# Rope of the second block: the rotation matmul replaced by four quarter evictions on ScalarE

## The reference, cut to what matters

```python
D_MODEL = 1024; SEQ = 256; ROT_DIM = 16
DA_HEADS = 8; DA_HEAD_DIM = 64; DIL_HEADS = 12; DIL_HEAD_DIM = 64

def partial_rope(t, cos, sin):
    half = ROT_DIM // 2
    t1, t2, tp = t[..., :half], t[..., half:ROT_DIM], t[..., ROT_DIM:]
    return jnp.concatenate([t1 * cos - t2 * sin, t2 * cos + t1 * sin, tp], axis=-1)

def second_block(x, positions, w_in, ...):
    cos, sin = rope_tables(positions, x.dtype)
    x = x + 0.5 * rmsnorm(swiglu(rmsnorm(x, g_pre_ffn1), w_gu1, w_down1), g_post_ffn1)
    h = rmsnorm(x, g_pre_mix)
    z = h @ w_in
    qa, ka, va, qd, kd, vd, ga, gb = jnp.split(z, cuts, axis=-1)   # 1024,1024,1024,768,768,768,1024,1024
    qa = partial_rope(qa.reshape(B, S, 2 * DA_HEADS, DA_HEAD_DIM), cos, sin)
    ka = partial_rope(ka.reshape(B, S, 2 * DA_HEADS, DA_HEAD_DIM), cos, sin)
    ...
    qd = partial_rope(qd.reshape(B, S, DIL_HEADS, DIL_HEAD_DIM), cos, sin)
    kd = partial_rope(kd.reshape(B, S, DIL_HEADS, DIL_HEAD_DIM), cos, sin)
    ...
```

## Time and profile before

| | |
|---|---|
| median of three runs | 1683.3 us (1682.68 to 1686.57) |
| the profiled execution, its own time | 1685.99 us |
| its span | 1684.2 us |
| TensorE (PE) busy | 1607.2 us, 95% |
| VectorE (DVE) busy | 1113.2 us, 66% |
| ScalarE (ACT) busy | 701.9 us, 42% |
| mean granted TensorE clock | 0.983 |

### The profile page before, as it was taken

One profiled execution on the slowest core, in us unless ns is written; L12 is line 12 of the kernel. 1 busy time (PEld: TensorE's weight loads), 2 busy tenths in 40 slices (PEclk: granted clock), 3 DMA queues, 4 the chain that ended last, 5 costly groups with the idle time before them and its releaser, 6 DMA issues.

```text
span 1684.2 us, 22878 instructions
## 1 busy us (share of the span) xinstructions
PE 1607.2 (95%) x9150; PEld 1334.4 (79%) x9150; DVE 1113.2 (66%) x1370; ACT 701.9 (42%) x889; POOL 53.0 (3%) x103
## 2 busy tenths in 40 slices
PE   6999999999999998999999999998999898889998
PEld 4655658888787877688999889997999787878887
DVE  4446526688888757457676788766664775557776
ACT  3425325222222236355444644344333554454343
POOL 1150000000000000000000000000000000000000
PEclk9999999999999999999999999998999999999999
DMA  9730462444565323113655566553555223426552
GB/s 394 282 116 1 157 225 75 150 150 152 182 240 200 125 75 100 51 57 133 202 176 186 163 201 198 176 189 103 157 159 173 93 77 100 161 77 206 192 182 92
DMA packets 168314, 258.16 MB, mean 153 GB/s; under 512 B 4176, under 2 KB 147024, under 8 KB 161456
## 3 DMA queue, kind: packets, MB, share of 16 engines
q1 hardware_dynamic: 160720, 205.21, 36.9%
q0 software_dynamic: 7376, 51.65, 8.2%
q10 hardware_dynamic: 144, 0.26, 0.1%
HBM read 256.05 MB, written 1.05 MB: 153 GB/s over the span
## 4 chain that ended last, share of the span: by engine, by line
PE 85%; issue 5%; DVE 4%; ACT 3%; DMA 2%; POOL 0%; DVEq 0%; SPq 0%; ACTq 0%
PE psum L355 52%; PE psum L375 14%; PE psum L379 7%; PE psum L476 2%; DMA U<-in_mod_pieces 1%; PE psum L1083 1%; PE psum L641 1%; DMA U<-in_w_mod 1%; PE psum L1124 1%; PE psum L2116 1%; PE psum L2388 1%; ACT w_hi L333 1%; PE psum L2367 1%; DVE scr L509 1%; PE psum L2200 1%
## 5 line engine op out<-in xcount | busy, mean ns | idle before, releaser
L337 DVE TENSOR_TENSOR w_lo<-w_raw,w_hi 128x2048 fp32r<-128x2048 f32 x189 | 432.8, 2290 | 184.9 <-ACT w_hi L333 183.3
L333 ACT ACTIVATE w_hi<-w_raw 128x2048 fp32r<-128x2048 f32 x189 | 360.8, 1911 | 260.0 <-PE psum L355 199.9
L355 PE MATMUL psum<-h_hi,w_hi 128*128 128x256 f32 (+1 forms) x1120 | 389.5, 348 | 19.9 <-DVE h_lo L522 9.3
L375 PE MATMUL psum<-h_hi,w_hi 128*128 128x512 f32 x1056 | 378.0, 401 | 11.9 <-DVE h_hi L490 7.6
L355 PE MATMUL psum<-h_lo,w_hi 128*128 128x256 f32 (+1 forms) x1120 | 375.9, 336 | 0.0
L355 PE MATMUL psum<-h_hi,w_lo 128*128 128x256 f32 (+1 forms) x1120 | 375.9, 336 | 0.0
L379 PE MATMUL psum<-h_hi,w_lo 128*128 128x256 f32 x1056 | 297.8, 282 | 0.0
L355 PEld LDWEIGHTS psum<-h_hi,w_hi 128*128 128x128 f32 x1120 | 216.8, 194 | 64.6 <-issue 33.5
L375 PEld LDWEIGHTS psum<-h_hi,w_hi 128*128 128x128 f32 x1056 | 200.0, 189 | 62.3 <-issue 14.0
L355 PEld LDWEIGHTS psum<-h_lo,w_hi 128*128 128x128 f32 x1120 | 217.2, 194 | 23.4 <-issue 4.1
L355 PEld LDWEIGHTS psum<-h_hi,w_lo 128*128 128x128 f32 x1120 | 216.8, 194 | 20.8
(11 more groups left out here) (294 smaller groups left out, 1703.0 us busy)
## 6 DMA issues: line engine op xcount, KB each, us to landing
w_raw<-in_ffn_w_up SPq DMA_DIRECT2D x44, 1024.0 KB, 5.1
w_raw<-in_w_gu SPq DMA_DIRECT2D x44, 1024.0 KB, 5.1
U<-in_w_mod POOLq DMA_DIRECT2D x40, 1024.0 KB, 5.5
w_raw<-in_w_in SPq DMA_DIRECT2D x29, 1024.0 KB, 5.3
w_raw<-in_ffn_w_down SPq DMA_DIRECT2D x22, 1024.0 KB, 5.0
w_raw<-in_w_down SPq DMA_DIRECT2D x22, 1024.0 KB, 5.0
U<-in_mod_pieces POOLq DMA_DIRECT2D x8, 1024.0 KB, 18.0
w_raw<-in_gqa_w_in SPq DMA_DIRECT2D x6, 1024.0 KB, 5.1
```

What stands on the lines that cost most here:

```text
L333: nc.scalar.activation(w_hi[:, i % RING, :], w_raw[:, i % RING, :], ACT.Copy).then_inc(hi_made, 1)
L337: nc.vector.tensor_tensor(w_lo[:, i % RING, :], w_raw[:, i % RING, :], w_hi[:, i % RING, :].bitcast(F32), ALU.subtract).then_inc(lo_made, 1)
L355: return [nc.tensor.matmul(dst, x, y, start=start and q == 0, stop=stop and q == 2, skip_group_check=True) for q, (x, y) in enumerate(pairs)]
L375: made = nc.tensor.matmul(psum[:, bank, :], wh, h_hi[:, k, :], start=k == 0, stop=False, skip_group_check=True)
```

## The change

The columns of the query and key weights are put in another order by the host (`qk_columns`): within each head of 64, numbers 0 to 7 stay at 0 to 7, numbers 16 to 39 come next, numbers 8 to 15 (the partners) go to places 32 to 39, and the rest follows. Partners are then exactly 32 partitions apart, and the exchange of partners is an exchange of neighbouring groups of 32 partitions. ScalarE makes it while it empties the PSUM bank: four instructions, each of 32 partitions x 512, which read group q ^ 1 and write group q of `scr`. The sign goes into the frequencies, so that the sine table is negative for one of the partners. VectorE then multiplies the bank itself by cosine (into `t_rope`), the swapped copy by sine, and adds. The matmul with `rot_b2` and its matrix in `const` are gone, VectorE handles stripe u in its own turn rather than one turn later, and the products go round six PSUM banks rather than four.

```diff
-    add("qkv", columns("w_in_2", 0, qk + v))
+    add("qkv", columns("qk_columns", 0, range(0, 3584, 256)) + columns("w_in_2", 0, v))
...
-        const = sb("const", [P, 5 * P + 8])
+        const = sb("const", [P, 4 * P + 8])
...
         def qkv_tensor(pe):
-            def turn(v):
-                pe.wait_ge(r_evac, v + 1)
-                need(pe, r_fix, 3 * (v - 1))
-                nc.tensor.matmul(psum[:, 4 + v % 2, :], rot_b2, t_rope[:, v % 2, :], start=True,
-                                 stop=True).then_inc(r_rot, 1)
-
...
-                need(pe, r_evac, u - 3)
+                need(pe, r_evac, u - 5)
+                need(pe, r_fix, 3 * (min(u - 6, N_ROT - 1) + 1))
                 for t in range(2):
-                    dst, done = psum[:, u % 4, block_cols(t)], r_sums if t else None
+                    dst, done = psum[:, u % 6, block_cols(t)], r_sums if t else None
...
-                if 1 <= u <= N_ROT:
-                    turn(u - 1)
 
         def qkv_scalar(act):
...
                 if u < N_ROT:
                     need(act, r_fix, 3 * (u - 1))
-                    nc.scalar.activation(t_rope[:, u % 2, :], psum[:, u % 4, :], ACT.Copy).then_inc(r_evac, 1)
+                    for q in range(4):
+                        made = nc.scalar.activation(scr[32 * q:32 * q + 32, u % 2, :],
+                                                    psum[32 * (q ^ 1):32 * (q ^ 1) + 32, u % 6, :], ACT.Copy)
+                    made.then_inc(r_evac, 1)
...
         def qkv_vector(dve):
...
-                if not 1 <= u <= N_ROT:
+                if u >= N_ROT:
                     continue
-                v = u - 1
-                dve.wait_ge(r_rot, v + 1)
-                need(dve, r_fix, 3 * v - 3)
-                x = t_rope[:, v % 2, :].rearrange("p (s t) -> p s t", s=2)
-                tmp = scr[:, v % 2, :].rearrange("p (s t) -> p s t", s=2)
-                nc.vector.tensor_tensor(tmp, bank2(4 + v % 2), double(tab_b2[:, 1, :]), ALU.mult).then_inc(r_fix, 1)
-                nc.vector.tensor_tensor(x, x, double(tab_b2[:, 0, :]), ALU.mult).then_inc(r_fix, 1)
-                dve.wait_ge(r_fix, 3 * v + 2)
-                nc.vector.tensor_tensor(qkv_dst(v), x, tmp, ALU.add).then_inc(r_fix, 1)
+                dve.wait_ge(r_evac, u + 1)
+                need(dve, r_fix, 3 * u - 3)
+                x = t_rope[:, u % 2, :].rearrange("p (s t) -> p s t", s=2)
+                other = scr[:, u % 2, :].rearrange("p (s t) -> p s t", s=2)
+                nc.vector.tensor_tensor(x, bank2(u % 6), double(tab_b2[:, 0, :]), ALU.mult).then_inc(r_fix, 1)
+                nc.vector.tensor_tensor(other, other, double(tab_b2[:, 1, :]), ALU.mult).then_inc(r_fix, 1)
+                dve.wait_ge(r_fix, 3 * u + 2)
+                nc.vector.tensor_tensor(qkv_dst(u), x, other, ALU.add).then_inc(r_fix, 1)
...
-            sp.dma_start(const[:, 0:5 * P + 3], a["const_base"]).then_inc(base_in, 16)
+            sp.dma_start(const[:, 0:4 * P + 3], a["const_base"]).then_inc(base_in, 16)
...
+    order = np.r_[0:8, 16:40, 8:16, 40:64]
+    qk_columns = np.concatenate([w_in_2[:, :, 0:2048], w_in_2[:, :, 3072:4608]], 2)
+    qk_columns = qk_columns.reshape(1, D, -1, 64)[:, :, :, order].reshape(1, D, -1)
```

More of the change, by code:

```diff
@@ L75, in stripes @@
     add("ffn2", ffn("w_gu1_2", "w_down1_2", 0))
-    qk = [*range(0, 2048, 256), *range(3072, 3840, 256), *range(3840, 4608, 256)]
     v = [*range(2048, 3072, 256), *range(4608, 5376, 256)]
-    add("qkv", columns("w_in_2", 0, qk + v))
+    add("qkv", columns("qk_columns", 0, range(0, 3584, 256)) + columns("w_in_2", 0, v))
     gate_b = columns("w_in_2", 0, range(6400, 7424, 256))
@@ L122, in build @@
         rinv = sb("rinv", [P, TT])
-        const = sb("const", [P, 5 * P + 8])
-        group_sum = const[:, 5 * P + 1:5 * P + 3]
+        const = sb("const", [P, 4 * P + 8])
+        group_sum = const[:, 4 * P + 1:4 * P + 3]
         par = sb("par", [P, 4, P])
@@ L132, in build @@
         ident, ones = const[:, 0:P], const[:, P:2 * P]
-        rot_mla, rot_gqa, rot_b2 = (const[:, i * P:(i + 1) * P] for i in (2, 3, 4))
-        inv_freq = const[:, 5 * P:5 * P + 1]
+        rot_mla, rot_gqa = (const[:, i * P:(i + 1) * P] for i in (2, 3))
+        inv_freq = const[:, 4 * P:4 * P + 1]
         eps, eps_down = small_w[:, 0:1], small_w[:, 1:2]
@@ L2140, in qkv_scalar @@
                     need(act, r_fix, 3 * (u - 1))
-                    nc.scalar.activation(t_rope[:, u % 2, :], psum[:, u % 4, :], ACT.Copy).then_inc(r_evac, 1)
+                    for q in range(4):
+                        made = nc.scalar.activation(scr[32 * q:32 * q + 32, u % 2, :],
+                                                    psum[32 * (q ^ 1):32 * (q ^ 1) + 32, u % 6, :], ACT.Copy)
+                    made.then_inc(r_evac, 1)
                 else:
-                    nc.scalar.activation(qkv_dst(u), bank2(u % 4), ACT.Copy).then_inc(r_evac, 1)
+                    nc.scalar.activation(qkv_dst(u), bank2(u % 6), ACT.Copy).then_inc(r_evac, 1)
         def qkv_vector(dve):
@@ L2738, in shape_constants @@
     f = np.float32
-    base = np.zeros((P, 5 * P + 3), f)
+    base = np.zeros((P, 4 * P + 3), f)
     base[:, 0:P] = np.eye(P)
     base[:, P:2 * P] = 1
-    rot = np.zeros((3, P, P), f)
+    rot = np.zeros((2, P, P), f)
     for which, rows in ((0, range(NOPE, MLA_QK, 2)), (1, range(0, P, 2))):
@@ L2745, in shape_constants @@
             rot[which, r + 1, r], rot[which, r, r + 1] = -1, 1
[L2746 to L2749, removed]
+    base[:, 2 * P:4 * P] = rot.transpose(1, 0, 2).reshape(P, 2 * P)
     inv = f(500000.0) ** (-(np.arange(0, 16, 2, dtype=f) / f(16)))
     for r in range(P):
-        if r % 64 < 16:
-            base[r, 5 * P] = inv[r % 8]
+        if r % 32 < 8:
+            base[r, 4 * P] = inv[r % 8] if r % 64 >= 32 else -inv[r % 8]
     def tables(dim, first, rows):
@@ L2774, in shape_constants @@
         if r % 32 < 2:
-            base[r, 5 * P + 1 + r % 32] = 1
+            base[r, 4 * P + 1 + r % 32] = 1
     return {
@@ L2808, in laid_out @@
     w_uq = np.asarray(inputs["mla_w_uq"][0], np.float32).reshape(QR, MLA_H, MLA_QK)
+    w_in_2 = np.asarray(inputs["w_in_2"], np.float32)
+    order = np.r_[0:8, 16:40, 8:16, 40:64]
+    qk_columns = np.concatenate([w_in_2[:, :, 0:2048], w_in_2[:, :, 3072:4608]], 2)
+    qk_columns = qk_columns.reshape(1, D, -1, 64)[:, :, :, order].reshape(1, D, -1)
     query_columns = np.concatenate([w_uq[:, :, :NOPE].reshape(QR, -1), w_uq[:, :, NOPE:].reshape(QR, -1)], 1)
     return {"x_columns": tokens.T.reshape(KD, P, TT).transpose(1, 0, 2), "parameters": parameters,
-            "query_columns": query_columns,
+            "query_columns": query_columns, "qk_columns": qk_columns,
             "mod_pieces": w_mod.transpose(3, 1, 0, 2, 4).reshape(KD, P, KD, T), "mix_stripes": np.stack(stripes_in)}
```

## The result

The changed kernel takes 1672.38 us (median of four runs, 1671.19 to 1673.09) against 1684.62 us for the kernel before, run beside it (four runs, 1682.68 to 1686.57). The ratio is 0.9927, with a 95% interval of [0.9909, 0.9944]: 0.7% faster, 12.2 us by the medians. The forecast was 1671.2 us, within 1667.5 to 1675.5.

A forecast was written before the change was run, and what follows sets the result against it. TensorE was taken to bound the stage, without gaps. Turns 11.9 us plus constants 0.15 us gave 12.05 us off the 1683.3 us median: 1671.2 us, range 1667.5 to 1675.5.

The forecast's parts named there:

- The turns: Fp32 rotation matmuls on TensorE between the rope stripes: 14 at 0.850 us, so removing them saves 11.9 to 12.0 us.
- Four evictions at 0.60 us, covered: ScalarE's PSUM copies per rope stripe go from 0.60 to 2.4 us, hidden under TensorE's 5.757 us stripe, 1.44 us idle.
- slow crossings: Rival: ScalarE evictions that read one partition group and write another are slow; no change 0.04 (with turns off path), slower 0.03.
- The cover's end at 0.96 us per eviction: Threshold in the rope stripes: TensorE's stripe stops covering ScalarE's work at (5.757 - 1.92) / 4 = 0.96 us per eviction.
- ScalarE as the bound: Rival case in the rope stripes: slow evictions make ScalarE's work per stripe, not TensorE's, set the stage's length.
- the first rival of slow crossings: Crossing evictions take 1.20 us, ScalarE 6.72 us per stripe: 1684.7 us, no change; 0.04 together with turns off the path.
- `w_lo` 4.6 us ahead: VectorE's `w_lo` for a stripe three further on is complete 4.6 us before TensorE wants it, against 8.8 before.
- Banks, loads, tables at nothing: Six PSUM banks, loads of stripes from `qk_columns` and earlier need of rope tables were each costed at nothing.
- The constants, 0.15 us: At the kernel's start, a first transfer smaller by 64 KB saves 0.15 us, between 0 and 0.2.
- The sum on the median, 12.05 us: Total gain 11.9 + 0.15 us, taken off the 1683.3 us median rather than the profiled run, giving 1671.2 us.
- The clock behind the stage, 0, and 3 us either way: Rival: TensorE clock falls after the stage shift; against, gain 5 to 9 us, 0.05; with, over 15 us, 0.02.

The follow-up runs named there:

- e1: The changed kernel with 14 plain fp32 128x512 matmuls put back at the places of the turns, waited for by nobody; 1684.31 us, ratio 0.9987.
- e2: The changed kernel with one 128x512 eviction per stripe in place of four of 32x512, rope partners not exchanged; 1673.77 us, ratio 0.9922.
- e3: The changed kernel with eight 32x512 evictions per stripe instead of four; 1683.63 us, ratio 0.9983.
- e4: The changed kernel with six 32x512 evictions per stripe instead of four; 1672.90 us, ratio 0.9916.
- e6: The changed kernel with products going round two PSUM banks rather than six; 1671.32 us, ratio 0.9929.
- e7: The changed kernel with the first constants transfer at its old size, 321.5 KB, the added part unused; 1674.42 us, ratio 0.9932.
- the second set: The runs of e5 to e8 on one chip: the kernel before took 1684.42 us, the changed kernel run again 1672.90 us.
- e5: The changed kernel itself, run again without edits; 1672.90 us, ratio 0.9931 to the kernel before.
- e11: The changed kernel with two more 32x512 evictions reading and writing the same groups as the fourth; one run, 1670.31 us, beside 1681.70 for the kernel before.
- e8: The changed kernel with the same exchange made in the first block's grouped attention, removing six rotation matmuls; 1670.54 us, ratio 0.9915.

## Why the prediction was right

- **The turns, 11.9 to 12.0 us.** Right. Taking them out brought the stage to 121.19 us, or 123.60 with a low clock at its start, and putting them back (e1) gave 135.48. 135.48 - 123.60 = 11.9 us between two stages with the same start.
- **Four evictions at 0.60 us, covered.** Right: 0.588 us each, 2.39 for four, 1.43 us left against 1.44 forecast. Crossing groups of partitions costs nothing over the 590 ns of the nearest row. The prediction says that no row shows such a crossing, and there it misread its own rows: half of the eight evictions of L1014 read partitions 64 to 127 of a bank and write partitions 0 to 63 of `q_mla`, a crossing by 64 places rather than 32, and all eight take 590 to 595 ns. With that row read, slow crossings deserved less of a chance than the prediction gave them. e2 shows that the four evictions are free, and e3 and e4 that this is so by the stripe's cover and has an end.
- **The cover's end at 0.96 us per eviction, 3.84 us per stripe.** Bracketed by e4 (3.59, free) and e3 (4.80, 10.8 us slower). So ScalarE as the bound is a real mechanism, and only the duration that it needed was not there. Its price was put too high, though: e3 has just the 4.80 us per stripe of the first rival of slow crossings, for which the prediction added up 14 stripes and came to 1.6 us above the kernel before. Measured are 132.01 us for the stage against 132.8 before at full clock, 0.8 us below, since the first three stripes lived on what `w_lo` had to spare.
- **`w_lo` 4.6 us ahead.** It was 4.8, as the rope took 1.95 us up to the next `w_lo` and not 2.13; e3 used it up in three stripes.
- **Banks, loads, tables at nothing.** Right for the banks (e6). Stripes from `qk_columns` landed after 5.0 us, those of `w_in_2` after 5.3, far inside the cover.
- **The constants, 0.15 us.** The traces speak for about that much, and the totals don't show it (e7).
- **The sum on the median, 12.05 us.** 12.2 by the medians of the first runs; the second set gives 1684.42 - 1672.90 = 11.5. That the first lies within 0.2 us of the forecast is luck: the interval of the ratio runs from 9.4 to 15.3 us.
- **The clock behind the stage, 0, and 3 us either way.** The bounds held; the middle was not quite 0. Lengths in the traces, in us, and the time at which the stage begins:

| trace | stage begins | stage | behind it |
|---|---|---|---|
| kernel before | 1168.31 | 135.46 | 380.4 |
| e1, turns back | 1168.68 | 135.48 | 380.5 |
| changed kernel, first | 1168.68 | 121.19 | 380.5 |
| changed kernel, e5 | 1168.15 | 123.60 | 379.1 |
| e2, e4, e6, e7, e11 | 1165.67 to 1171.41 | 123.6 | 379.0 to 379.3 |

Behind the stage the code is the same in all of these, and in six of the seven traces with a short stage that part is 1.1 to 1.4 us shorter than in the kernel before. From the start of the stage to the end the gain is then 13.0 to 13.3 us, and 14.2 by the first trace. The larger spread is one that the prediction did not name: it lies ahead of the stage, 5.7 us from trace to trace with the same instructions, and the change does not touch it. The prediction expected low clock at the start of the stage in the trace after; the first trace had none, which made the stage's gain look 2.4 us larger than it is.

- **A miscount.** The chain of the earlier trace rows has 14 turns, and 13 pieces of 5.75 us between them, not 14 of each. The period is worked out over 13, and nothing else rests on it.

## What to carry to other kernels

Where one engine is busy without a gap, an operation on it is worth its full time, and its price is the difference of the periods with and without it; work moved to another engine is free as long as that engine's sum per period stays under the period of the first (here free at 5.51 of 5.757 us, and not at 6.72), so work out that threshold before, and try a dose above and below it afterwards. A partial tile costs ScalarE as much as a full one, and that matters only on an engine near the bound. Before calling something untried, look through the kernel's own rows for it: a crossing eviction was among them. Where a removed operation gives back less than its time, as in e8, follow the chain to the next wait: here ScalarE came to end last, and work for later stood ahead of work for now in two in-order queues. Moving that work gave 3.4 us by the ratios, no less than the six removed matmuls had given (2.7).

## What the runs showed of the hardware

Reading one group of 32 partitions and writing another costs ScalarE nothing in its duration: 588 ns for 32 x 512, the 128 x 512 copy takes 598. What it loses is the overlap with its neighbour: behind a whole-width eviction the next instruction starts after 0.49 us (e2), but four evictions of four different groups start 0.60 us apart, and so do the rounding behind them and all six of e4. With the same group three times in a row the overlap is back (e11). The Trainium skill, in "ScalarE: Activation LUTs", section What ACT_TABLE_LOAD costs, has ACTIVATEs back to back overlap by about 93 ns; the 0.10 to 0.11 us here are near that where the start partition stays, and where it changes there is no such overlap.

An execution of one and the same program can enter a stage at either clock level after the same wait of 3.4 us: 1.00 in one trace, 0.53 in another, 2.4 us apart in the length of the stage. A difference of that size between two single traces is no evidence until the granted clock has been read beside it.
